# Another group order, another row stride and another operand schedule in the projection stage of a hybrid attention layer

## The chip, the core and the metric

The kernel runs on one core of a Trainium2 chip. The metric is the device time of one execution in microseconds (us). The core has five engines that run their own instruction streams and meet at semaphores: TensorE (PE, matrix products; PEld is its weight load), VectorE (DVE), ScalarE (ACT), GpSimd (POOL) and SyncE (SP), which here only issues DMA transfers. Sixteen DMA engines move the data of all transfers.

## The reference, cut to what matters

```python
def reference(x, mem, pre_norm, w_in, sink_a, mem_norm, w_mem_kv, w_out, post_norm):
    u = rms_norm(x, pre_norm)                         # (4096, 1024)
    proj = einsum('bsd,de->bse', u, w_in)             # 1024 x 3072 weights
    qa, ka, va, ga, qb, kb, vb, gb, qc, gc = split(proj, IN_SPLITS)
    # A: 6 query heads, 2 key heads, causal window 128, a sink; partial rotary on 16 of 64 dims
    # B: 6 heads, causal windows (128, 1), (512, 4), (2048, 16) as (window, dilation); partial rotary
    # C: 4 heads over 256 memory tokens, no rotary
    qa, ka, qb, kb = apply_partial_rope(...)
    ...
    y = concatenate([oa * silu(ga), ob * silu(gb), oc * silu(gc)])
    y = einsum('bse,ed->bsd', y, w_out)
    return x + rms_norm(y, post_norm)
```

All is float32, one batch, 4096 tokens, width 1024. The change touches only the first line's norm and the projection `proj`, with its rotary part and the way in which the results reach DRAM.

## The kernel before, in words

Three stages follow one another: `project_stage` (norm, projection, rotary), `attend_stage` and `finish_stage`. The first ends at 1211 us of the profiled span, and only it is changed.

**Tiles.** The stage goes through the tokens in four quarters of 1024 and, in each quarter, through the twelve groups of 256 output channels that the table `PAIRS` lists. A group is named by kind: G gate channels, R the 16 rotated dimensions of eight heads at a time (query and key), P the rest of these heads' dimensions, L those of the last four heads (rotated and not), C queries of group C, V values. Before, the order is G0 R0 G1 P0 P1 P2 L0 C0 V0 V1 G2 G3. In the text the place of a group in the quarter is i = 0 to 11, its number over all quarters is g.

**Seven products.** A group is a 256 x 1024 by 1024 x 1024 product, done as a 2 x 2 block product with seven block products instead of eight (slots j = 0 to 6). Product j multiplies an operand of the weights, W_j, and one of the tokens, U_j. U_0, U_3 and U_5 are blocks of the input, U_1, U_2, U_4 and U_6 are sums and differences that `add_u` makes in place, and U_j stays for the whole quarter. W_1, W_2, W_4 and W_5 are sums that POOL makes in the first quarter, when they are also stored to `scratch_w_s` and loaded from there in later quarters. Every operand is split into a high and a low part (`high_w`, `high_u` on ACT; `low_w`, `low_u` on DVE), and a product is 4 x 3 = 12 matmuls 128 x 128 by 128 x 512 (L807 to L809). The seven accumulate in three PSUM banks; ACT copies twice (`ps`, L477, and `p5`, L482) and DVE joins twice (L690, L695) between them. The four result blocks are called 11, 22, 12 and 21 (channel tile, token chunk).

**What sets the order.** All engines run a loop `slot(g, j)`, written out in their own code, and an engine does its work of a slot in the order of that code. `high_w(m + 2)` and `low_w(m + 2)` stand two slots ahead of their product, three buffers deep. The tables `ACT_AT` and `DVE_AT` say in which slot after a group's start its result blocks are copied to `out_a` (ring of four, ACT) and `out_b` (ring of two, DVE: `low`, L584, and the rotary steps `shuffle`, `straight`, `across`, `both`, L600 to L620). SP stores each block one slot later (`store_a`, `store_b`), and `claim_a` and `claim_b` make ACT and DVE wait until the ring's old contents have landed in DRAM. Blocks of R, P, L go to `scratch_qk_hi` and `scratch_qk_lo`, each as one DMA, or two for L, through `rows_to`. A V block is turned on PE (`turn_v`) and stored by nine DMAs (L307, L311, L314).

**The next quarter's tokens.** From i = 2 to i = 9 one tile of 128 tokens of the next quarter goes through: SP loads it to `x_next` in slot 4 of the group before (L364), ACT squares it in slot 0 (L419), DVE and ACT make the scale (`mean`, `root`, `invert`, slots 1 and 2; L562, L423, L567), ACT scales it (`scale`, slot 2, L427), PE turns it in slot 3 (L779) and DVE keeps it in slot 4 (L574). In group 11 the seven operands are replaced: `add_u` for n = 0, 1 in slots 1 and 2 of group 10, n = 2, 3 in slots 1 and 4 of group 11, `high_u` and `low_u` (L414, L546) of U_0 to U_5 in slots 1 to 6, of U_6 in slot 0 of the next quarter. Ahead of the first quarter all of this stands before slot 0.

**Last quarter.** There are no next tokens; the 256 memory tokens go through in groups 1 to 5, `differ` makes four sums of the output weights at `DIFFER_AT`, and POOL loads the first head's queries and keys when the stores are through.

## Time and profile before

| | us |
|---|---|
| median of 3 runs | 2367.25 |
| lowest and highest | 2360.48, 2370.09 |
| the profiled execution | 2361.82 |
| its span, first to last instruction | 2360.0 |
| projection stage in it | 0 to 1211 |

The page of the profile gives PE as busy for 89% of the span, PEld 74%, DVE 65%, ACT 57%, POOL 4%, and a granted TensorE clock of 0.936 on average. A matmul is pipelined, so a busy PE need not be at its peak; what counts below is how long a group of seven products takes from its first matmul to the next group's first. The timeline lists instructions in order of time with the idle time of their engine before them and what ended it; `x4` behind a row says how many alike are merged. `SPq` rows are issues of DMAs. The view of windows gives, for chosen stretches, busy times, the granted clock (1.00 is 2.4 GHz, 0.5 is 1.2 GHz) and the share of the 16 DMA engines that was busy.

### The profile page before, as it was taken

What the parts mean: (1) busy time and instruction counts of PE and PEld (TensorE: products, weight loads), DVE (VectorE), ACT (ScalarE), POOL (GpSimd) and SP (SyncE); (2) the same over time, 40 slices, a digit from 0 to 9 for tenths busy, and PEclk for the clock granted to TensorE, in tenths of its full rate; (3) what the DMA queues carried; (4) which work ended last, traced back from release to release, by engine and by line L of the source; (5) the groups of instructions that cost most, each with busy time, mean ns of one, the idle gap of its engine ahead of it and who ended that gap; (6) DMA issues with size and microseconds to landing.
All of it is one profiled execution on the core that took longest, in us unless ns stands there. A gap on an engine that the chain in (4) does not pass through costs nothing. (4 is left out here: it accounts for less than half of the span.)

```text
span 2360.0 us, 39321 instructions
## 1 busy us (share of the span) xinstructions
PE 2107.9 (89%) x12892; PEld 1754.0 (74%) x12892; DVE 1544.9 (65%) x4410; ACT 1353.5 (57%) x3520; POOL 93.1 (4%) x92
## 2 busy tenths in 40 slices
PE   4997879979899798997869999999999979899998
PEld 3776668767687576876758888888778868678886
DVE  6534455443654435534338889899889968788887
ACT  6442445534554345422249988899779969633332
POOL 0211120000000000000110000000000000000000
PEclk6998999989999899999978999899999989999999
DMA  4464565656566466565867767866959878345553
GB/s 135 151 203 155 176 199 157 218 162 195 174 189 211 151 198 198 163 230 187 239 160 142 141 121 139 165 120 129 173 115 219 198 179 214 118 161 166 168 163 124
DMA packets 429816, 401.39 MB, mean 170 GB/s; under 512 B 202128, under 2 KB 327184, under 8 KB 424768
## 3 DMA queue, kind: packets, MB, share of 16 engines
q1 hardware_dynamic: 424656, 377.38, 60.2%
q0 software_dynamic: 4976, 21.71, 2.9%
q8 instruction: 97, 1.59, 0.3%
q14 instruction: 87, 0.71, 0.1%
HBM read 255.62 MB, written 143.39 MB: 169 GB/s over the span
## 5 line engine op out<-in xcount | busy, mean ns | idle before, releaser
L807 PE MATMUL p_ps<-p_u_hi,p_w_hi 128*128 128x512 f32 x1344 | 548.2, 408 | 91.0 <-DVE p_w_lo L539 26.1
L808 PE MATMUL p_ps<-p_u_lo,p_w_hi 128*128 128x512 f32 x1344 | 537.6, 400 | 0.0
L809 PE MATMUL p_ps<-p_u_hi,p_w_lo 128*128 128x512 f32 x1344 | 537.2, 400 | 0.0
L539 DVE TENSOR_TENSOR p_w_lo<-p_w_raw,p_w_hi 128x512 fp32r<-128x512 f32 x336 | 240.1, 719 | 361.5 <-ACT p_w_hi L403 359.8
L1567 ACT ACTIVATE probs<-probs,a_stat 128x256 f32<-128x256 f32 (+1 forms) x896 | 433.7, 489 | 51.8 <-DVE a_stat L1401 48.9
L403 ACT ACTIVATE p_w_hi<-p_w_raw 128x512 fp32r<-128x512 f32 x336 | 209.1, 626 | 358.8 <-PE p_ps L809 344.9
L807 PEld LDWEIGHTS p_ps<-p_u_hi,p_w_hi 128*128 128x128 f32 x1344 | 262.4, 195 | 155.8 <-issue 58.3
L1401 DVE CUSTOM_DVE_ANT_0 probs<-a_ps_s,fixed 128x256 f32<-128x256 f32 (+1 forms) x704 | 251.8, 397 | 87.8 <-PE a_ps_s L1300 86.3
L809 PEld LDWEIGHTS p_ps<-p_u_hi,p_w_lo 128*128 128x128 f32 x1344 | 261.0, 194 | 57.1
L808 PEld LDWEIGHTS p_ps<-p_u_lo,p_w_hi 128*128 128x128 f32 x1344 | 261.9, 195 | 53.1
L1354 PE MATMUL a_ps_o<-a_pT,a_v 128*64 128x128 f32 x3320 | 259.5, 288 | 23.3 <-ACT a_pT L1591 21.7
L1370 PE MATMUL a_ps_t<-fixed,probs 128*128 128x128 f32 x1660 | 262.8, 280 | 6.3 <-ACT a_pT L1591 4.6
L1490 DVE TENSOR_SCALAR probs<-probs,a_coef 128x256 f32<-128x256 f32 (+1 forms) x896 | 263.6, 339 | 3.0
L1591 ACT ACTIVATE a_pT<-a_ps_t 128x512 f32<-128x512 f32 (+1 forms) x412 | 229.7, 561 | 40.6 <-PE a_ps_t L1370 40.3
L1354 PEld LDWEIGHTS a_ps_o<-a_pT,a_v 128*64 128x64 f32 x3320 | 184.5, 139 | 80.2 <-ACT a_pT L1591 45.3
L1299 PE MATMUL a_ps_s<-k_hi,q 128*128 128x256 f32 (+1 forms) x672 | 218.6, 343 | 7.2 <-PEq L248 3.5
L1370 PEld LDWEIGHTS a_ps_t<-fixed,probs 128*128 128x128 f32 x1660 | 197.8, 144 | 13.8 <-DVE probs L1490 8.1
L1300 PE MATMUL a_ps_s<-k_lo,q 128*128 128x256 f32 (+1 forms) x672 | 193.2, 304 | 0.0
L1567 ACT ACTIVATION_READ_ACCUMULATOR probs<-probs,a_stat 128x1 f32 x896 | 175.0, 195 | 0.0
L1299 PEld LDWEIGHTS a_ps_s<-k_hi,q 128*128 128x128 f32 x672 | 138.1, 205 | 37.2 <-issue 27.3
L2168 PE MATMUL f_ps<-f_w_lo,parts_hi 128*128 128x512 f32 x384 | 150.1, 391 | 0.0
L2167 PE MATMUL f_ps<-f_w_hi,parts_hi 128*128 128x512 f32 x368 | 144.5, 393 | 5.4 <-DVE probs L2083 4.1
(200 smaller groups left out, 2748.5 us busy)
## 6 DMA issues: line engine op xcount, KB each, us to landing
p_w_raw<-in_w_in SPq DMA_DIRECT2D x156, 256.0 KB, 3.9
p_w_raw<-scratch_w_s SPq DMA_DIRECT2D x144, 256.0 KB, 3.7
scratch_qk_hi<-p_out_a SPq DMA_DIRECT2D x80, 256.0 KB
scratch_qk_lo<-p_out_b SPq DMA_DIRECT2D x80, 256.0 KB
a_v<-scratch_v SPq DMA_DIRECT2D x40, 512.0 KB, 7.4
scratch_gate<-p_out_a SPq DMA_DIRECT2D x64, 256.0 KB
scratch_v<-p_out_a SPq DMA_DIRECT2D x256, 64.0 KB
a_gate<-scratch_gate SPq DMA_DIRECT2D x64, 256.0 KB, 5.1
```

Of the source, the lines that this page charges most:

```text
L403: nc.scalar.activation(w_hi[:, m % 3, :, :], w_raw[:, entry(j, g), :, :], ACT.Copy).then_inc(w_hi_ready, 1)
L539: nc.vector.tensor_tensor(w_lo[:, m % 3, :, :], w_raw[:, entry(j, g), :, :], w_hi[:, m % 3, :, :].bitcast(F32), ALU.subtract).then_inc(w_l ...
L807: nc.tensor.matmul(bank, hi, u_hi[j][:, k, :], start=j < 2 and k == 0, stop=False, skip_group_check=True)
L808: nc.tensor.matmul(bank, hi, u_lo[j][:, k, :], start=False, stop=False, skip_group_check=True)
L809: last = nc.tensor.matmul(bank, lo, u_hi[j][:, k, :], start=False, stop=k == KH - 1, skip_group_check=True)
L1299: nc.tensor.matmul(out, w, keys_of(keys_hi, u), start=True, stop=False)
L1354: last = nc.tensor.matmul(place_of(ps_o[j * HD:(j + 1) * HD, bank % 2, :], u), v[name][:, half, tile, :], pT[:, e % 4, j, at * P:(at + 1) ...
L1370: last = nc.tensor.transpose(ps_t[:, e % 2, j, at * P:(at + 1) * P], probs[:, s, 2 * e + j, at * P:(at + 1) * P], ident[:])
L1401: last = nc.vector.tensor_tensor_reduce(out=probs[:, s, 2 * slot + j, a:], in0=ps_s[:, slot % NS, j, a:], in1=masks[u.kind][:, a:], scale= ...
L1490: last = nc.vector.tensor_scalar(place, place, coef[:, s, u.column:u.column + 1], None, ALU.mult)
L1567: last = nc.scalar.activation(place, place, ACT.Exp, scale=-1.0, bias=stat[:, s, 0, u.column:u.column + 1], accum_out=stat[:, s, 1, u.colu ...
L1591: nc.scalar.activation(pT[:, e % 4, :, a[0]:], ps_t[:, e % 2, :, a[0]:], ACT.Copy).then_inc(turned_copied, 1)
```

## The change

1. `PAIRS` becomes G0 V0 R0 G1 P0 P1 V1 L0 P2 C0 G2 G3: the two V groups stand at i = 1 and i = 6, five groups apart, and C at i = 9. `DIFFER_AT` moves by one to two groups, and `turn_v` waits for the tiles of its own place.
2. In `rows_to` the rows of the qk scratch tensors are addressed as `(a q) n`, one stride of four rows, where they were `(h q r) n`, blocks of 16 rows. Row 4a + part holds what row 64h + 16 part + r held, for queries and keys alike, so that the dimensions of a head stand in another order in all of them. The readers are unchanged.
3. The token operands are replaced at slots 1, 3, 4, 6, 7, 9 and 10 from the start of group 11 (`U_AT`), seven operands over eleven products, on DVE one slot later; `add_u` moves with them. The square of the next tile stands in slot 6 of the group before instead of slot 0, its mean and inverse one slot earlier.
4. In the first group of all the products run in the order 0 3 1 2 4 5 6 (`FIRST`), and U_0 and U_3 are split before the last tiles are through. `number`, `u_number` and `product_at` carry that order to the semaphores.

```diff
-PAIRS = (("G", 0), ("R", 0), ("G", 1), ("P", 0), ("P", 1), ("P", 2), ("L", 0), ("C", 0), ("V", 0), ("V", 1), ("G", 2), ("G", 3))
+PAIRS = (("G", 0), ("V", 0), ("R", 0), ("G", 1), ("P", 0), ("P", 1), ("V", 1), ("L", 0), ("P", 2), ("C", 0), ("G", 2), ("G", 3))
...
-        DIFFER_AT = ((7, 6), (8, 1), (8, 4), (8, 6))
+        DIFFER_AT = ((8, 6), (9, 1), (9, 4), (9, 6))
...
+        FIRST = (0, 3, 1, 2, 4, 5, 6)
+        U_AT = {1: 0, 3: 1, 4: 2, 6: 3, 7: 4, 9: 5, 10: 6}
+
+        def product_at(g, place):
+            return FIRST[place] if g == 0 else place
+
+        def number(g, j):
+            return NJ * g + (FIRST.index(j) if g == 0 else j)
...
                     if kind == "L":
-                        by = of[2 * 512:2 * 512 + 256].rearrange("(h q r) n -> q h r n", q=4, r=16)
-                        return [(slice(HD * e, HD * e + HD), by[2 * t + e][:, :, cols]) for e in range(2)]
+                        by = of[2 * 512:2 * 512 + 256].rearrange("(a q) n -> q a n", q=4)
+                        return [(slice(HD * e, HD * e + HD), by[2 * t + e][:, cols]) for e in range(2)]
...
-                    by = of[512 * i:512 * i + 512].rearrange("(h q r) n -> q h r n", q=4, r=16)
-                    return [(slice(0, P), by[part][:, :, cols])]
+                    by = of[512 * i:512 * i + 512].rearrange("(a q) n -> q a n", q=4)
+                    return [(slice(0, P), by[part][:, cols])]
...
-                for j in (4, 6, 0, 3):
+                for j in (0, 3, 4, 6):
                     load_w(j, 0)
...
-                        act.wait_ge(raw_ready, XT * quarter + (4 if quarter == 0 and j == 0 else XT))
+                        act.wait_ge(raw_ready, XT * quarter + (4 if quarter == 0 and j < 5 else XT))
...
-                    if t == 5:
-                        high_u(0, 0)
-                for j in range(1, NJ):
+                    if t in (5, 6):
+                        high_u(0, FIRST[t - 5])
+                for j in FIRST[2:]:
                     high_u(0, j)
...
-                    if i == NP - 1 and quarter < 3 and j > 0:
-                        high_u(quarter + 1, j - 1)
-                    if i == 0 and 0 < quarter < 4 and j == 0:
-                        high_u(quarter, NJ - 1)
+                    if i == NP - 1 and quarter < 3 and j in U_AT:
+                        high_u(quarter + 1, U_AT[j])
+                    if i == 0 and 0 < quarter < 4 and NJ + j in U_AT:
+                        high_u(quarter, U_AT[NJ + j])
...
+                    if quarter < 3 and 0 <= t + 1 < XT and j == 6:
+                        n = (quarter + 1) * XT + t + 1
+                        act.wait_ge(x_loaded[0], 16 * (n - XT + 3))
+                        square(n, x_next)
                     if quarter < 3 and 0 <= t < XT:
                         n = (quarter + 1) * XT + t
-                        if j == 0:
-                            act.wait_ge(x_loaded[0], 16 * (n - XT + 3))
-                            square(n, x_next)
...
-                    if quarter < 3 and i == NP - 2 and j in (1, 2):
-                        add_u(quarter + 1, j - 1)
-                    if quarter < 3 and i == NP - 1 and j > 0:
-                        low_u(quarter + 1, j - 1)
-                        if j == 1:
-                            add_u(quarter + 1, 2)
-                        if j == 4:
-                            add_u(quarter + 1, 3)
+                    if quarter < 3 and i == NP - 2 and j in (1, 4):
+                        add_u(quarter + 1, (1, 4).index(j))
+                    if quarter < 3 and i == NP - 1 and j - 1 in U_AT:
+                        low_u(quarter + 1, U_AT[j - 1])
+                    if quarter < 3 and i == NP - 1 and j == 3:
+                        add_u(quarter + 1, 2)
...
-                product(g, j)
+                product(g, product_at(g, j))
```

The order of instructions moves at three places that matter below.

**First place: SP around the value stores, second quarter.** `scratch_v` rows are the nine stores of a V block, `p_spare<-in_x` is the load of the next tile, `p_w_raw` rows are weight loads. Before, around the first block of V0:

```order
L323 DMA scratch_qk_lo<-p_out_b 128x512 [waits p_lo_ready]
L259 DMA p_w_raw<-scratch_w_s 128x512 [waits p_w_lo_ready] x2
L364 DMA p_spare<-in_x 128x1024 [waits p_u_turned]
L259 DMA p_w_raw<-in_w_in 128x512 [waits p_w_lo_ready] x2
L259 DMA p_w_raw<-scratch_w_s 128x512 [waits p_w_lo_ready]
L307 DMA scratch_v<-p_out_a 128x4x128 [waits p_a_ready]
L311 DMA scratch_v<-p_out_a 32x4x128 x4
L314 DMA scratch_v<-p_out_a 16x8x128 x4
```

After, around the last two blocks of V1, in group L0:

```order
L319 DMA scratch_v<-p_out_a 128x4x128 [waits p_a_ready]
L323 DMA scratch_v<-p_out_a 32x4x128 x4
L326 DMA scratch_v<-p_out_a 16x8x128 x4
L271 DMA p_w_raw<-scratch_w_s 128x512 [waits p_w_lo_ready]
L319 DMA scratch_v<-p_out_a 128x4x128 [waits p_a_ready]
L323 DMA scratch_v<-p_out_a 32x4x128 x4
L326 DMA scratch_v<-p_out_a 16x8x128 x4
L271 DMA p_w_raw<-scratch_w_s 128x512 [waits p_w_lo_ready]
L376 DMA p_spare<-in_x 128x1024 [waits p_u_turned]
L271 DMA p_w_raw<-in_w_in 128x512 [waits p_w_lo_ready]
L329 DMA scratch_qk_hi<-p_out_a 64x512 [waits p_a_ready]
L329 DMA scratch_qk_hi<-p_out_a 64x512
```

The last tile's load stood ahead of the value stores; now a tile's load stands behind four blocks of nine stores, after V0 and after V1. The stores of L have a two-dimensional row pattern, 64x512, where it was 4x16x512 (and 128x512 for R and P, where it was 8x16x512).

**Second place: ACT at the start of the program**, from the split of the token operands to the first copy of a product (`p_ps<-p_ps`). Before:

```order
L414 ACTIVATE p_u_hi1<-p_spare 128x2048 [waits p_added]
L414 ACTIVATE p_u_hi2<-p_raw 128x2048 [waits p_added]
L414 ACTIVATE p_u_hi3<-p_raw 128x2048 [waits p_raw_ready]
L414 ACTIVATE p_u_hi4<-p_raw 128x2048 [waits p_added]
L414 ACTIVATE p_u_hi5<-p_raw 128x2048 [waits p_raw_ready]
L414 ACTIVATE p_u_hi6<-p_raw 128x2048 [waits p_u_turned,p_added]
L403 ACTIVATE p_w_hi<-p_w_raw 128x512 [waits p_w_added]
L477 ACTIVATE p_ps<-p_ps 128x512 [waits p_multiplied]
```

After:

```order
L427 ACTIVATE p_u_hi3<-p_raw 128x2048 [waits p_raw_ready]
L436 ACTIVATE p_ss<-p_ss 128x1 [waits p_meaned]
L440 ACTIVATE p_x_first<-p_x_first,p_ss 128x1024 [waits p_inverted]
L427 ACTIVATE p_u_hi1<-p_spare 128x2048 [waits p_added]
L427 ACTIVATE p_u_hi2<-p_raw 128x2048 [waits p_added]
L427 ACTIVATE p_u_hi4<-p_raw 128x2048 [waits p_added]
L427 ACTIVATE p_u_hi5<-p_raw 128x2048 [waits p_raw_ready]
L427 ACTIVATE p_u_hi6<-p_raw 128x2048 [waits p_u_turned,p_added]
L416 ACTIVATE p_w_hi<-p_w_raw 128x512 [waits p_w_added]
L490 ACTIVATE p_ps<-p_ps 128x512 [waits p_multiplied]
```

U_3 moved ahead of the last tile's scale; the copy of product 0 still stands behind all seven splits. On PE the second product is now that of U_3, and its first row waits for that copy (`p_products_copied`), which product 1 did not.

**Third place: DVE at the change from the first to the second quarter**, from the split of U_1 on. Before:

```order
L546 TENSOR_TENSOR p_u_lo1<-p_spare,p_u_hi1 128x2048 [waits p_added,p_u_hi_ready]
L690 TENSOR_TENSOR p_ps<-p_ps,p_p5 128x512 [waits p_products_copied,p_multiplied]
L539 TENSOR_TENSOR p_w_lo<-p_w_raw,p_w_hi 128x512 [waits p_w_hi_ready]
L546 TENSOR_TENSOR p_u_lo2<-p_raw,p_u_hi2 128x2048 [waits p_added,p_u_hi_ready]
L539 TENSOR_TENSOR p_w_lo<-p_w_raw,p_w_hi 128x512 [waits p_w_hi_ready]
L546 TENSOR_TENSOR p_u_lo3<-p_raw,p_u_hi3 128x2048 [waits p_u_hi_ready]
L557 TENSOR_TENSOR p_raw<-p_raw 128x2048 [waits p_added]
L695 TENSOR_TENSOR p_c22<-p_ps,p_p5 128x512 [waits p_a_ready,p_multiplied]
```

After:

```order
L561 TENSOR_TENSOR p_u_lo1<-p_spare,p_u_hi1 128x2048 [waits p_added,p_u_hi_ready]
L713 TENSOR_TENSOR p_c22<-p_ps,p_p5 128x512 [waits p_a_ready,p_multiplied]
L554 TENSOR_TENSOR p_w_lo<-p_w_raw,p_w_hi 128x512 [waits p_w_hi_ready]
L561 TENSOR_TENSOR p_u_lo2<-p_raw,p_u_hi2 128x2048 [waits p_added,p_u_hi_ready]
L554 TENSOR_TENSOR p_w_lo<-p_w_raw,p_w_hi 128x512 [waits p_w_hi_ready] x2
L561 TENSOR_TENSOR p_u_lo3<-p_raw,p_u_hi3 128x2048 [waits p_u_hi_ready]
L554 TENSOR_TENSOR p_w_lo<-p_w_raw,p_w_hi 128x512 [waits p_w_hi_ready]
L561 TENSOR_TENSOR p_u_lo4<-p_raw,p_u_hi4 128x2048 [waits p_added,p_u_hi_ready]
```

Between U_1's split and the second join (`p_c22`) stood two more splits and a sum; now the join comes right behind it.

## Rows read from the trace of the kernel before

**Rows 1.** Windows, L807 alone: quarters one, two, four; length, PE busy, PEclk, DMA.

```profile
35.41:357.58 322.17, 140.30 (x336) 67.81 (x337) 0.89 0.52 164
357.58:632.99 275.41, 135.64 (x337) 64.65 (x336) 0.95 0.59 182
...
910.55:1211.40 300.85, 137.16 (x336) 65.14 (x335) 0.93 0.66 204
```

**Rows 2.** Windows, single groups: R0, G1, C0, C0 (last quarter), G3 three times.

```profile
376.65:395.69 19.04, 10.89 (x28) 5.26 (x28) 1.00 0.48 153
395.69:415.65 19.96, 10.99 (x28) 5.26 (x28) 1.00 0.59 169
499.41:534.12 34.71, 11.73 (x28) 5.69 (x28) 0.80 0.43 134
1070.67:1100.63 29.96, 11.75 (x29) 5.64 (x28) 0.83 0.42 128
601.67:632.99 31.32, 12.91 (x29) 6.08 (x28) 0.84 0.54 161
321.35:357.58 36.23, 12.47 (x28) 6.11 (x28) 0.86 0.65 196
1171.05:1211.10 40.05, 12.76 (x28) 6.17 (x28) 0.74 0.66 187
```

**Rows 3.** Windows, one product each, after a stall and at full clock.

```profile
524.40:528.68 4.28, 2.39 (x4) 1.30 (x5) 0.63 0.77 223
531.40:534.12 2.72, 1.56 (x4) 0.75 (x4) 1.00 0.75 242
```

**Rows 4.** Waits over the whole span: total us, times, longest us.

```profile
DVE p_out_b L584 <- DMA scratch_qk_lo<-p_out_b: 106.9, 34, 6.8
...
PE p_ps_t L779 <- ACT p_spare L427: 63.4, 15, 14.1
...
DVE p_out_b L608 <- DMA scratch_qk_lo<-p_out_b: 48.5, 4, 13.9
```

**Rows 5.** Timeline, group C0 of the second quarter: DVE, ACT, ACT, PE.

```profile
516.27 0.69 DVE L608 COPY p_out_b<-p_ps 64x512 f32<-64x512 f32 x1 [12.09 <-DMA scratch_qk_lo<-p_out_b]
...
518.35 0.20 ACT L423 ACTIVATE p_ss<-p_ss 128x1 f32<-128x1 f32 x1 [14.90 <-DVE p_ss L562]
...
521.58 1.15 ACT L427 ACTIVATE p_spare<-p_spare,p_ss 128x1024 f32<-128x1024 f32 x1 [2.02 <-DVE p_ss L567]
...
522.78 1.11 PE L779 MATMUL p_ps_t<-p_ident,p_spare 128*128 128x128 f32 x4 [12.32 <-ACT p_spare L427]
```

**Rows 6.** Windows, all engines: while P stores run, then while only L stores run.

```profile
445.00:447.00 2.00, 2.00 (x10) 1.67 (x9) 0.72 (x4) 1.21 (x3) 0.00 (x0) 1.00 0.53 197
...
512.00:514.00 2.00, 0.00 (x0) 0.00 (x0) 0.00 (x0) 0.00 (x0) 0.00 (x0) 0.97 0.26 102
```

**Rows 7.** Timeline of SP, third of the V blocks behind V0, second quarter.

```profile
570.59 0.59 SPq L259 DMA_DIRECT2D p_w_raw<-in_w_in  x1
571.23 0.43 SPq L307 DMA_DIRECT2D scratch_v<-p_out_a  x1
...
573.77 2.46 SPq L314 DMA_DIRECT2D scratch_v<-p_out_a  x4
```

**Rows 8.** Page, DMA issues: count, KB each, median us to landing.

```profile
p_spare<-in_x SPq DMA_DIRECT2D x24, 512.0 KB, 4.2
```

**Rows 9.** Timeline of the program's start: DVE, DVE, ACT, PE.

```profile
52.72 6.69 DVE L546 TENSOR_TENSOR p_u_lo<-p_raw,p_u_hi 128x2048 fp32r<-128x2048 f32 x3
59.33 1.89 DVE L539 TENSOR_TENSOR p_w_lo<-p_w_raw,p_w_hi 128x512 fp32r<-128x512 f32 x3
...
52.84 1.91 ACT L414 ACTIVATE p_u_hi<-p_raw 128x2048 fp32r<-128x2048 f32 x1 [1.49 <-DVE p_raw L557]
...
60.12 0.77 PE L807 MATMUL p_ps<-p_u_hi,p_w_hi 128*128 128x512 f32 x1 [9.27 <-DVE p_w_lo L539]
```

**Rows 10.** Timeline of ACT in the last group of the stage.

```profile
1191.63 0.60 ACT L444 ACTIVATE p_out_a<-p_ps 128x512 f32<-128x512 f32 x1 [15.84 <-DMA scratch_v<-p_out_a]
```

68 lines of the change are left out of this document (39 added, 29 removed).

## The prediction

> **What bounds the kernel now.** I read the windows first, a quarter at a time and then a group at a time, because the busy share of PE says little about a stage with many short stalls. A group without anything beside its seven products takes 19.04 us, 2.72 us a product, and one that also turns a tile of the next tokens takes 19.96 us, both at a granted clock of 1.00 [rows 2]. Twelve groups, eight of them with a tile, are 12 x 19.04 + 8 x 0.92 = 235.8 us, and the turning of the two V groups' blocks adds an estimated 4 us, so that an undisturbed quarter is about 240 us. The quarters took 322, 275 and, the last one, 301 us [rows 1]; the third was like the second. Some 14 us of the last are the memory tokens' own products. So about 205 us of the 1176 us from the first product to the end are stalls and the slow clock behind them, and PE is what waits. In the stretches of single groups most of this sits at three places: C0 (35 us in the second quarter, 30 in the last, where 19 to 20 would do), G3 (31, 36 and 40 us) and the start [rows 2, 9]. The two other stages are not changed, and their 1149 us are taken as they are.
>
> A stall costs more than its length: the product after one took 4.28 us at a mean clock of 0.63, where the next but one took 2.72 at 1.00 [rows 3]. I add 1.6 us to each stall over about 2 us.
>
> **Part 1, the row stride.** In C0 PE waits 12.32 us for ACT's scale of the next tile, ACT has waited 14.90 us for DVE's mean, and DVE 12.09 us for the buffer whose last content, an L block's low part, was still on its way to DRAM [rows 5]. Why it was: in a stretch in which only L stores run, 0.26 of the DMA engines' time is busy, 4.2 of sixteen engines, at 102 GB/s, which is 24 GB/s an engine; with P stores it is 0.53, 8.5 engines [rows 6]. The patterns had 4 and 8 as their outer size. Half an L block is 128 KB, so four engines take 1.35 us for it, an L group's 16 halves 21.5 us, all on the same four, issued within some 14 us. With 64 or 128 rows as the outer size I take sixteen engines: 128 KB in 0.34 us, a P block in 0.67 us instead of 1.33. The Trainium skill, "DMA: Bandwidth & Descriptors", section "Why a DMA increments its semaphore by 16 and not by 1", says that a transfer is split over the largest number up to 16 that divides the outer size on both sides; the trace agrees for the 4 and the 8, and by that rule the new patterns get 16, while by the bounds of rows 6 alone they get between 4 and 16. Two sums come off. The four C0 groups exceed their floor by 15, 14.8, 15 and 10.9 us (36 less 20, and so on), 56 us, of which two are in rows 2. The other waits of the turn: 63.4 us in 15 waits, less three in C0 of 14.1, 12.3 and about 12, leave 25 [rows 4, 5]; with the clock behind six of them 35. DVE's 107 us of short waits for these stores [rows 4] are what fed them, and the earlier square and mean (one slot, 2.72 us) help the same chain; I leave 6 us of the 35. Gain: 56 + 29 = 85 us, if nothing takes the place of the waits.
>
> **Part 2, the value groups apart.** A V block is nine DMA issues: from 571.23 to 576.23 SP issues nothing else, and with the weight load ahead of it a block takes 5.7 us of SP [rows 7]. A slot is 2.72 us. Eight blocks in a row put SP some 20 us behind, and G3 pays: in the last quarter ACT waits 15.84 us there for a V block's store, and G3 takes 40 us for 19 [rows 10, 2]. I put the lag's share at 22 us there, 10 in the first quarter, 7 each in the two between (the rest of their excess is part 3). Behind a single V group SP lags about as far at its end but has catch-up time before a ring is full. Gain: 46 us.
>
> What it triggers: SP now loads a tile behind the four blocks (the first order excerpt). The first block is issued about 2 us before the following group begins, four blocks and four weight loads are 22.8 us, so the tile's load is issued at about 21.5 us into that group and lands 4.2 us later [rows 8], at about 26. ACT's square of it stands in slot 6, at about 18 us, and ACT is in order: queued behind it are the weight splits and the copy that product 2 of the next group needs. That product would start at about 26.5 us; it gets its copy at 26 + 1.1 (square) + 1.7 to 2.3 (a split, one or two block copies, the copy itself) = 29 to 29.5. Stall 3 us and the clock, 4 to 5 us, at six places: R0 and L0 of three quarters. In the first quarter the weight sums are not loaded by SP, the lag is 2 us shorter, and R0 costs 1. In L0 the lag meets a second wait: L's first low block is stored about 29 us into the group, and DVE wants its buffer at 25.5 until it lands at 32. The two overlap; I take 5 us for L0 in each of four quarters and 4, 4 and 1 for R0. Cost: 29 us. Bounds: 0, if SP drains in time, and 65, if each of the seven costs the 9 us by which the wait for a slow landing could grow.
>
> **Part 3, seven operands over eleven products.** A split of an operand is 6.69 / 3 = 2.2 us on DVE, a weight split 0.63, and 1.9 us on ACT [rows 9]. Before, seven splits and two sums, nine times 2.2, with seven weight splits and two joins (5.7 us), are 25.5 us of DVE in 19 us of G3: 6.5 us too much. That agrees with G3's 31.3 less 19.0 less the 7 of part 2. Over the ten slots from 2 to 11 the same nine, ten weight splits and four joins are 28.7 us in 27.2, and DVE may run 4 us late on the weight splits. The joins have 2 us of slack. The first two splits and the sum push the second join about 1 us past it, so I leave 2 us at each of three changes. Gain: 19 - 6 = 13 us.
>
> **Part 4, the start.** DVE's chain ahead of slot 0 stays what it was: seven splits, four sums, eight tiles, and the third product began at 60.12 when it was through [rows 9]. The split of U_3 fills 2 us in which DVE waited for the last tile, but U_2's high part now stands between two of DVE's steps and costs them back. The second product needs the copy of product 0, which ACT reaches only after all seven splits (second excerpt), at about 58.4: product 1 ran at 46 to 50 before, product 3 cannot now. It takes 4.5 us at half clock, so the third product starts at 63 instead of 60, and the join of product 1 comes one slot nearer. The rest catches nothing up but DVE's own lag of 1 us. Cost: 2 us, between 0 and 5.
>
> **Edits at no cost.** The memory tokens' ACT wait in group 1 of the last quarter stays, now in V0. `differ` moves to P2 and C0, whose DVE has 0.7 us more work a slot; its own spacing is the same, and so is its wait for the transfers; up to 3 us if that cover is gone. The permuted rows are read in the same whole rows by the later stages.
>
> **Sum.** 85 + 46 + 13 - 29 - 2 = 113 us off the profiled execution's 2361.82: 2249 us. The median of the three runs is 5.4 us above that execution; with half of it for the changed kernel's median I predict 2251 us.
>
> **Rivals.** *The tile loads are in time.* If SP's lag is a few us shorter or the stores, now on all engines, land sooner, the square does not wait and L0 costs half: 26 us less, 2225 us. For it: the weight loads in rows 7 are only one a block. Against it: nothing shortens the nine issues. *The tile loads cost double.* With ACT blocked, a split, a copy and the join come late one after another, as in G3 before: 29 more, 2280 us. *The stores do not spread*, or rows 64 KB apart are written more slowly than rows 16 KB apart: the change does not do what it says. Then the 85 us stay away and only parts 2 to 4 count: 46 + 13 - 2 - 9 (R0) = 48, 2314 us. For it: no row before shows such a row distance; against it: with an outer size of 8 the engines kept 24 GB/s each at rows 1 MB apart between engines. *Slower than before.* The new ACT wait for a tile's load at the six places is the mechanism. The gains without it are 142 us; to be over by 12 us it has to cost over 25 us a place, so a tile would land about 48 us into the group. It decides if the weight loads behind the same lag arrive late as well, so that PE waits first for them and SP for PE's weights again: 27 us a place gives 2362 - 142 + 162 = 2382 us. Against it: in G3, with twice as many blocks, the whole excess was 12 to 21 us.
>
> **Chances.** The forecast 0.58, tiles in time 0.18, tiles double 0.13, no spread 0.08, slower 0.03. About 12 us, 0.5%, is what a measurement of this kernel can tell from no change. All cases but the last are faster by more; I leave 0.02 for a sum of small losses that ends level. The range is 2212 to 2292: it takes in the first three cases with some 12 us for the sizes of parts 1 and 2, and leaves out the no-spread case.
>
> **What would show it.** Part 1: windows with L stores at a DMA share well over 0.26; DVE's waits for `scratch_qk_lo` from 155 us to under 50; PE's waits for ACT's scale under 15 us; C0 near 20 us. Part 2: G3 of the last quarter near 20 us, and in its place a wait of ACT's square (now L432) for `p_spare<-in_x` in R0 and L0 of 5 to 8 us, six times. Part 3: G3 and the G0 behind it together near 40 us, with PE's idle time there by the join. Part 4: the second product at 58 us, group 0 ending near 77. The quarters would be near 278, 254, 254 and 271 us. Wrong would be a DMA share that stays at 0.26 under L stores, or no wait of ACT for tiles, or G3 still over 25 us.

## The result, and the profile after

| | before | after |
|---|---|---|
| median of 4 runs | 2363.86 us | 2241.4 us |
| lowest and highest | 2357.76, 2370.09 | 2240.56, 2245.04 |
| the profiled execution | 2361.82 | 2240.56 |
| its span | 2360.0 | 2238.8 |
| first product to last product of the projection | 35.4 to 1211.6 | 35.5 to 1084.5 |

The ratio of after to before is 0.9485, 95% interval 0.9455 to 0.9515: 122 us or 5.2% faster. The prediction was 2251 us, range 2212 to 2292. All twelve runs below are timed beside the kernel before; its median in the three sets was 2365.5, 2363.2 and 2364.5 us, the last without one execution of 2439.65 us that had a lower granted clock (0.82) and stands in no ratio.

Line numbers have moved, and each run below has those of its own kernel. In the changed kernel the square is L432, the mean L577, the reciprocal L582, ACT's scale L440, PE's turn of a tile L797, `straight` L623, `low` L599, the copy of product 0 L490, the join L708.

The first view is of windows, with the matmuls of L825 alone: length, busy PE, busy PEld, granted clock, DMA share, GB/s. The rows are the four quarters; then C0 of the second and of the last quarter; G3 of the second and of the last; G1 and P2 of the second, P2 of the third and of the first.

```profile
35.52:315.50 279.98, 135.90 (x337) 65.03 (x337) 0.95 0.58 186
315.50:564.94 249.44, 133.90 (x337) 63.78 (x336) 0.99 0.65 203
564.94:815.84 250.90, 133.99 (x336) 63.79 (x336) 0.99 0.64 201
815.84:1084.10 268.26, 134.65 (x336) 64.11 (x335) 0.97 0.70 224
506.42:526.35 19.93, 10.98 (x28) 5.26 (x28) 1.00 0.80 263
1025.08:1045.54 20.46, 10.97 (x29) 5.25 (x28) 1.00 0.82 298
545.39:564.94 19.55, 10.97 (x29) 5.26 (x28) 1.00 0.46 139
1065.34:1084.10 18.76, 10.89 (x28) 5.07 (x27) 1.00 1.02 253
376.23:398.06 21.83, 11.07 (x28) 5.25 (x28) 1.00 0.73 228
479.76:506.42 26.66, 12.34 (x29) 5.94 (x28) 0.87 0.73 227
731.33:757.30 25.97, 11.78 (x28) 5.56 (x28) 0.93 0.73 232
224.88:255.43 30.55, 12.32 (x28) 6.00 (x28) 0.89 0.69 196
```

Read beside [rows 1, 2]: C0 went from 34.7 and 30 us to 19.9 and 20.5, G3 from 31.3 and 40 to 19.6 and 18.8, both at full clock. The quarters took 280, 249, 251 and 268 us where the prediction had 278, 254, 254 and 271. Group 0 of the first quarter takes 41.3 us, and in the last quarter V0 takes 27.4 and P0 32.9 us beside the work on the memory tokens, much as R0 and P1 did before (26.7 and 32.9 us). What else is left over the 19.96 us of a plain group with a tile sits in P2 (6 to 10.6 us, in every quarter) and in G1 (5.4, 1.9 and 4.0 us in the first three). These are the two groups that follow R0 and L0, and R0 and L0 are the groups that follow the single V groups.

The second view is of the waits over the whole span: total us, times, longest.

```profile
ACT p_spare L432 <- DMA p_spare<-in_x: 37.7, 8, 7.4
DVE p_out_b L599 <- DMA scratch_qk_lo<-p_out_b: 42.0, 20, 4.6
DVE p_out_b L623 <- DMA scratch_qk_lo<-p_out_b: 22.3, 4, 8.7
PE p_ps_t L797 <- ACT p_spare L440: 4.0, 2, 3.0
PE p_ps L825 <- ACT p_ps L490: 34.5, 7, 18.8
```

DVE's waits for the low parts' stores fell from 155 us [rows 4] to 64, PE's waits for a scaled tile from 63.4 to 4.0, and ACT no longer waits for the stores of V blocks ([rows 10] had 15.84 us of it in one place). In their place stands ACT's wait for the next tile, 37.7 us, of which 37.0 are the six waits behind the V groups, 4.0 to 7.4 us each.

The third view is the timeline around L0 and P2 of the second quarter (P2 begins at 479.76): the fourth V block and the tile's load on SP, ACT's square, PE's third product of P2, DVE's ring. SPq L319, L323 and L326 are the nine issues of a V block.

```profile
474.31 0.43 SPq L319 DMA_DIRECT2D scratch_v<-p_out_a  x1
474.78 2.02 SPq L323 DMA_DIRECT2D scratch_v<-p_out_a  x4
476.85 4.05 SPq L326 DMA_DIRECT2D scratch_v<-p_out_a  x4
480.95 0.59 SPq L271 DMA_DIRECT2D p_w_raw<-scratch_w_s  x1
481.58 0.44 SPq L376 DMA_DIRECT2D p_spare<-in_x  x1
...
484.83 1.13 SPq L335 DMA_DIRECT2D scratch_qk_lo<-p_out_b  x2
485.29 1.06 ACT L432 ACTIVATE p_spare<-p_spare 128x1024 f32<-128x1024 f32 x1 [7.36 <-DMA p_spare<-in_x]
...
487.86 0.58 ACT L490 ACTIVATE p_ps<-p_ps 128x512 f32<-128x512 f32 x1
...
488.59 0.77 PE L825 MATMUL p_ps<-p_u_hi,p_w_hi 128*128 128x512 f32 x1 [3.23 <-ACT p_ps L490]
...
493.53 0.69 DVE L623 COPY p_out_b<-p_ps 64x512 f32<-64x512 f32 x1 [3.82 <-DMA scratch_qk_lo<-p_out_b]
```

The tile is loaded 22.9 us after L0 began (the prediction said 21.5, and a landing at 26; ACT's square starts as it lands, 26.6 us after), ACT's in-order queue holds the split and the copy behind the square, and PE stalls 3.23 us (the prediction said 3), then runs this product and the next at a lower clock. At the end of the stage stands something that the prediction left out. The timeline has POOL's first load of the next stage's queries and PE's first matmul of that stage, behind a barrier:

```profile
1059.78 0.53 POOL L933 DMA_DIRECT2D q<-scratch_qk_hi  x1 [11.48 <-DMA scratch_qk_lo<-p_out_b]
...
1092.88 0.44 PE L1318 MATMUL a_ps_s<-k_hi,q 128*128 128x128 f32 x1 [8.33 <-PEq L260]
```

The barrier opens when all engines are through, and the last are SP and POOL: the last gate store landed at 1091.9 us and the last of POOL's loads at 1091.2. Both share the DMA engines (the DMA share over G3 is 1.02). SP's last wait ahead of the barrier, in the view of its waits, is for those stores:

```profile
SPq L399 <- DMA scratch_gate<-p_out_a: 6.4, 1, 6.4
```

### The profile page after: what moved, and what is told of

It is laid out like the page before. It is cut to its first block and busy times, and to the rows that moved or that the text cites. A ratio compares the mean times of both kernels' runs of the same rounds, so it can differ in the third digit from the quotient of the medians.

```text
span 2238.8 us, 39324 instructions
## 1 busy us (share of the span) xinstructions
PE 2071.6 (93%) x12892; PEld 1730.7 (77%) x12892; DVE 1546.8 (69%) x4410; ACT 1352.4 (60%) x3520; POOL 95.8 (4%) x92
## 5 line engine op out<-in xcount | busy, mean ns | idle before, releaser
L825 PE MATMUL p_ps<-p_u_hi,p_w_hi 128*128 128x512 f32 x1344 | 538.4, 401 | 53.9 <-ACT p_ps L490 34.5
L827 PE MATMUL p_ps<-p_u_hi,p_w_lo 128*128 128x512 f32 x1344 | 530.1, 394 | 0.0
L826 PE MATMUL p_ps<-p_u_lo,p_w_hi 128*128 128x512 f32 x1344 | 529.7, 394 | 0.0
L825 PEld LDWEIGHTS p_ps<-p_u_hi,p_w_hi 128*128 128x128 f32 x1344 | 256.8, 191 | 114.8 <-DVE p_w_lo L554 26.9
L827 PEld LDWEIGHTS p_ps<-p_u_hi,p_w_lo 128*128 128x128 f32 x1344 | 256.2, 191 | 55.1
L826 PEld LDWEIGHTS p_ps<-p_u_lo,p_w_hi 128*128 128x128 f32 x1344 | 256.9, 191 | 51.3
L1373 PE MATMUL a_ps_o<-a_pT,a_v 128*64 128x128 f32 x3320 | 259.1, 288 | 22.5 <-ACT a_pT L1610 20.7
```

What stands on the lines that cost most here:

```text
L825: nc.tensor.matmul(bank, hi, u_hi[j][:, k, :], start=j < 2 and k == 0, stop=False, skip_group_check=True)
L826: nc.tensor.matmul(bank, hi, u_lo[j][:, k, :], start=False, stop=False, skip_group_check=True)
L827: last = nc.tensor.matmul(bank, lo, u_hi[j][:, k, :], start=False, stop=k == KH - 1, skip_group_check=True)
L1373: last = nc.tensor.matmul(place_of(ps_o[j * HD:(j + 1) * HD, bank % 2, :], u), v[name][:, half, tile, :], pT[:, e % 4, j, at * P:(at + 1) ...
```

## The experiments

**Part 1 alone.** The kernel before with the two new lines of `rows_to`.

```diff
-    by = of[2 * 512:2 * 512 + 256].rearrange("(h q r) n -> q h r n", q=4, r=16)
-    return [(slice(HD * e, HD * e + HD), by[2 * t + e][:, :, cols]) for e in range(2)]
+    by = of[2 * 512:2 * 512 + 256].rearrange("(a q) n -> q a n", q=4)
+    return [(slice(HD * e, HD * e + HD), by[2 * t + e][:, cols]) for e in range(2)]
```

> The kernel before with part 1 alone: the blocks of R, P and L go to rows of one stride, the order of the groups, the operands and the start are those of before. My theory (the stores of L ran on four engines and held DVE's ring, which made the square's mean, ACT's scale and PE's turn late): C0 of the middle quarters falls from 34.7 us to about 20, the DMA share while L blocks are stored rises over 0.5, and the time is 2362 less 56 (C0) less 25 to 40 (the other waits for a scaled tile) = 2266 to 2281 us. Rival (L directly ahead of C0 is what costs, whatever the rate, because each L block is two transfers and the ring has two places): C0 stays at 25 us or more, and no more than 60 us are gained, 2302 us or more.

Measured: 2281.64 us (2275.95 to 2283.14), ratio 0.9633 (0.9583 to 0.9682). 84 us are gained, and the time is 0.6 us over the range that I expected; the prediction had 85 for this part. Windows, all engines, of C0 in the second quarter, and 2 us inside it in which L blocks are stored (the last three numbers are clock, DMA share, GB/s):

```profile
466.62:491.68 25.06, 21.77 (x94) 17.84 (x92) 12.65 (x23) 10.57 (x19) 0.00 (x0) 0.93 0.64 191
...
471.00:473.00 2.00, 2.00 (x11) 1.65 (x10) 0.38 (x1) 0.00 (x0) 0.00 (x0) 1.00 0.92 306
477.00:479.00 2.00, 0.66 (x3) 0.20 (x2) 1.24 (x3) 0.73 (x2) 0.00 (x0) 1.00 0.00 0
```

With a weight load beside the L stores the DMA share is 0.92 at 306 GB/s, where [rows 6] had 0.26 at 102, and a few us later nothing is in flight. In the changed kernel there is a stretch in which the transfers in flight are L stores alone:

```profile
490.60:491.79 1.19, 1.19 (x5) 0.91 (x4) 0.00 (x0) 0.00 (x0) 0.00 (x0) 0.50 0.85 257
```

The stretches of [rows 6] were not quite that. In the one with P stores two weight loads were in flight, and in the one with L stores one, which had been issued behind the L stores at 506.86 us and landed only at 516.85, 10.0 us later. The weight load behind L stores in the run with part 1 alone took 3.0 us (472.35 to 475.32). So transfers that fill a few DMA engines also hold up a later one that needs those engines among others.

C0, however, stays at 25 us, as the rival said: DVE still waits 3.05 us for the ring there, with the mean behind it. Over its four groups C0 gives 37 us (8.1, 9.7, 9.7, 9.6) where I had 56, and the other groups give 46 where I had 29. Each theory was right about one of the two.

**Part 1 undone.** The changed kernel with the old lines of `rows_to`, the diff above reversed.

> The changed kernel with the row stride of before (outer size 4 for L, 8 for R and P), all else as changed. My theory: the waits for the low parts' transfers come back behind L0, P2 and C0 wait for scaled tiles, and 50 to 85 us of the gain go: 2290 to 2325 us, with a DMA share of 0.26 while only L blocks are stored. Rival (the new order of groups alone, with P2 between L0 and C0, gives DVE the time that it lacked): under 25 us are lost, 2265 us or less.

Measured: 2346.96 us (2340.72 to 2357.99), ratio 0.9928 (0.9902 to 0.9954). 106 us are lost, over the upper end of what I expected, and the kernel is within 1% of the one before. Windows of P2 in the second quarter, and 2 us inside it:

```profile
524.61:562.70 38.09, 24.54 (x93) 19.71 (x92) 11.50 (x21) 11.02 (x20) 0.00 (x0) 0.78 0.45 151
543.00:545.00 2.00, 0.00 (x0) 0.00 (x0) 0.00 (x0) 0.00 (x0) 0.00 (x0) 0.51 0.26 102
```

P2 takes 43.5, 38.1, 37.0 and 36.8 us, C0 28, 24, 25 and 31. No engine works in that window: the four DMA engines hold everything. DVE's wait at L623 is 61.3 us in four places (22.3 in the changed kernel). The stride is worth more in the new order than in the old (106 us against 84). My reading is that L0 now stands behind a V group and its stores begin late as well; no run parts this from the rest. This run is also the case "the stores do not spread" of the prediction, which priced it at 2314 us. Without part 1 the other parts bring some 18 us and not the 48 of that case.

**Same rows, another pattern.** The changed kernel with the same addresses written as two sizes.

```diff
-    by = of[2 * 512:2 * 512 + 256].rearrange("(a q) n -> q a n", q=4)
-    return [(slice(HD * e, HD * e + HD), by[2 * t + e][:, cols]) for e in range(2)]
+    by = of[2 * 512:2 * 512 + 256].rearrange("(h r q) n -> q h r n", q=4, r=16)
+    return [(slice(HD * e, HD * e + HD), by[2 * t + e][:, :, cols]) for e in range(2)]
```

> The changed kernel with every block going to exactly the same rows as in it, but with the rows written as a pattern of two sizes, 4 x 16 for L and 8 x 16 for R and P, instead of 64 and 128. If the number of engines follows the outer size of the pattern, the DMA share under L stores is 0.26 again and the time is that of the kernel with the old stride within 5 us (2290 to 2325). If it follows the addresses, or the two sizes are merged on the way, the time is that of the changed kernel, 2241 within 5 us.

Measured: 2245.77 us (2237.88 to 2248.41), ratio 0.948 (0.9429 to 0.953), the changed kernel's 0.9485. Two microseconds with L stores in P2 show 0.97 of the DMA engines busy:

```profile
488.00:490.00 2.00, 1.64 (x8) 1.02 (x6) 0.00 (x0) 1.24 (x3) 0.00 (x0) 1.00 0.97 336
```

Weight loads are in flight beside them here too. So it is not how the pattern is written in the source that counts, but whether the rows lie at one distance. Whether two sizes of one stride are merged before the transfer is issued, or the split goes by the addresses, this run can't tell.

**Part 2 undone.** The old group order in the changed kernel.

```diff
-PAIRS = (("G", 0), ("V", 0), ("R", 0), ("G", 1), ("P", 0), ("P", 1), ("V", 1), ("L", 0), ("P", 2), ("C", 0), ("G", 2), ("G", 3))
-DIFFER_AT = ((8, 6), (9, 1), (9, 4), (9, 6))
+PAIRS = (("G", 0), ("R", 0), ("G", 1), ("P", 0), ("P", 1), ("P", 2), ("L", 0), ("C", 0), ("V", 0), ("V", 1), ("G", 2), ("G", 3))
+DIFFER_AT = ((7, 6), (8, 1), (8, 4), (8, 6))
```

> The changed kernel with the group order of before (V0 and V1 side by side ahead of G2, L0 ahead of C0), all else as changed: part 2 undone alone. My theory: SP's lag comes back in G3, 22, 10, 7 and 7 us (46 in all), C0 behind L0 costs 25 us again as with the stride alone (5, 5 and 8 over its floor, 18 us), and the stalls in G1 and P2 behind the single V groups go (35 us by the trace of the changed kernel): 2241 + 46 + 18 - 35 = 2270 us, between 2258 and 2282. Rival (setting the V groups apart moves the same SP lag from G3 to R0 and L0 and wins nothing): 2246 us or less, with G3 over 25 us and G1 and P2 at 20.

Measured: 2252.57 us (2248.13 to 2254.43), ratio 0.9532 (0.9507 to 0.9556): 11 us slower than the changed kernel, between the two expectations. As a time that is no more than a measurement here can tell; the groups of the two traces say where it sits. Windows, all engines, of G3 in the last, first, second and third quarter, then C0 of the second:

```profile
1060.21:1099.60 39.39, 21.57 (x83) 17.00 (x84) 5.55 (x8) 7.87 (x14) 10.63 (x15) 0.78 0.67 188
284.83:317.03 32.20, 22.36 (x85) 17.67 (x85) 16.64 (x14) 15.85 (x20) 5.91 (x4) 0.79 0.67 209
539.74:563.67 23.93, 21.17 (x86) 16.74 (x84) 14.05 (x13) 14.46 (x18) 0.00 (x0) 0.93 0.64 201
785.46:811.04 25.58, 21.13 (x85) 16.73 (x84) 14.06 (x13) 14.48 (x18) 0.00 (x0) 0.93 0.65 196
455.67:476.98 21.31, 20.39 (x94) 16.55 (x93) 11.52 (x21) 10.61 (x19) 0.00 (x0) 1.00 0.78 222
```

G3 costs 20.6, 12.6, 4.4 and 6.0 us more than in the changed kernel, 43.6 in all (46 predicted), and G1 and P2 cost 43 us less. So SP's lag was moved and not removed, and both sides are of one size. The rest that makes the new order win is small: C0 behind L0 costs 4.4 and 1.4 us in the first two quarters, V0 of the last quarter, where the four sums collide with it, 7 us; and 5 us go back at the end of the stage, which the old order passes in 3.5 us and the new one in 8.3.

**Part 3 undone.** The operands replaced one a slot again.

```diff
-U_AT = {1: 0, 3: 1, 4: 2, 6: 3, 7: 4, 9: 5, 10: 6}
+U_AT = {1: 0, 2: 1, 3: 2, 4: 3, 5: 4, 6: 5, 7: 6}
```

with `low_u` in the same slot as `high_u` and the sums at their old places.

> The changed kernel with the operands of the next quarter replaced as before, one a slot in G3 and the last in slot 0 of G0: part 3 undone alone. My theory (DVE has 25.5 us of work in 19 us of G3): G3 goes from 19.6 us to 24 to 26 at the three changes of quarter, G0 behind it from 19.8 to 19.0, and the time is 2241 + 3 x 5 = 2256 us, between 2251 and 2262. Rival (the stalls in G3 were SP's lag alone, and with that gone DVE's extra work hides in the slack ahead of the joins): 2245 us or less.

Measured: 2260.55 us (2253.51 to 2264.89), ratio 0.9573 (0.954 to 0.9607); its profiled execution has a span of 2254.9 us, 16 more than the changed kernel's. Windows of G3 and of the G0 behind it:

```profile
554.69:579.87 25.18, 21.21 (x86) 16.76 (x85) 20.69 (x16) 17.49 (x19) 0.00 (x0) 0.93 0.35 97
579.87:598.90 19.03, 19.03 (x85) 15.76 (x84) 10.87 (x12) 9.57 (x16) 0.00 (x0) 1.00 0.57 175
```

5.6 us in G3 less 0.8 in G0, three times, are 14.4 us (13 predicted), with 3.5 more in G2 of the first quarter and 0.4 in each of the other two. DVE is busy 20.7 of the 25.2 us, and PE waits for its joins (2.89 and 1.08 us). The theory holds.

**Part 4 undone.** The start of before: `FIRST = (0, 1, 2, 3, 4, 5, 6)`, the splits and sums in their old order, the weights loaded in the order 4, 6, 0, 3.

> The changed kernel with the start of before (products 0, 1, 2, 3 in that order in group 0, the splits and sums in their old order, the weight blocks loaded in the old order): part 4 undone alone. My prediction put part 4 at a cost of 2 us, between 0 and 5: 2239 us, with the second product at 46 us, the third at 60 and group 0 ending at 75. Rival (the new order helps what follows group 0): 2244 us or more.

Measured: 2239.5 us (2238.28 to 2245.02), ratio 0.9481 (0.9458 to 0.9504). The second and third products start at 45.5 and 59.3 us and group 0 ends at 75.0, as expected; it takes 40.4 us (41.3 in the changed kernel). Parts of 2 us can't be told from no change here; that it costs 2 us agrees with the prediction and is not shown.

**The tile's load moved forward.** `load_next` is the load of the tile as it was, made a function.

```diff
+    if g < G and j == 2 and g and kind_of(g - 1) == "V":
+        load_next(g)
     ... the stores of the slot ...
-    if quarter < 3 and 0 <= t < XT and j == 4:
+    if j == 4 and not (g and kind_of(g - 1) == "V"):
         load_next(g)
```

> The changed kernel with one issue moved on SP: behind a V group (in R0 and L0) the next tile is loaded in slot 2, between the second and the third V block, instead of in slot 4 behind all four. My theory (ACT's square waits for that load, 37.7 us in 8 waits, and the copy that PE needs is queued behind it): the square waits no more, G1 falls from 25.4, 21.8 and 23.9 us to 20, P2 from 30.6, 26.7 and 26.0 to 22 to 24, where the wait of DVE for the ring of L stays; 2241 - 22 = 2219 us, between 2211 and 2227. Rival (SP's lag of four blocks is what costs, through the weight loads and the ring of L as well; another wait takes the place of this one): under 10 us, 2231 us or more.

Measured: 2258.58 us (2256.68 to 2269.6), ratio 0.9555 (0.9501 to 0.9608). It is 17 us slower than the changed kernel. Another wait took the place of the one removed, as the rival had it, but neither expectation had a loss. Timeline of L0 and P2 in the second quarter (P2 begins at 491.78): PE's turn of the tile before, the load behind it, L's first low block, DVE's wait for the ring:

```profile
482.73 1.03 PE L804 MATMUL p_ps_t<-p_ident,p_spare 128*128 128x128 f32 x8
483.80 0.36 SPq L365 DMA_DIRECT2D p_spare<-in_x  x1
...
500.66 1.11 SPq L335 DMA_DIRECT2D scratch_qk_lo<-p_out_b  x2
...
508.04 0.69 DVE L630 COPY p_out_b<-p_ps 64x512 f32<-64x512 f32 x1 [11.50 <-DMA scratch_qk_lo<-p_out_b]
```

ACT no longer waits for a tile. But the tile's buffer is free only when PE has turned the tile before, so SP stood still for 3 us with two V blocks behind it, L's first low block went out 29.9 us after L0 began instead of 26.1, and DVE's wait for the ring grew from 3.8 to 11.5 us. P2 took 31.2 us instead of 26.7, and now the scale waits for the reciprocal behind that ring.

**The load ahead of the fourth block only, the scale's inputs first.** The same edit at `j == 3`, by when PE has turned the tile, and on DVE:

```diff
+    if g < G and quarter < 3 and 0 <= i - X_AT < XT:
+        if j == 0:
+            mean((quarter + 1) * XT + i - X_AT)
+        if j == 1:
+            invert((quarter + 1) * XT + i - X_AT)
     for age in (2, 1, 0):
```

> The changed kernel with two edits against the stalls in G1 and P2: the tile behind a V group is loaded in slot 3, ahead of the fourth V block only (PE has turned the tile before it by then, so SP need not wait as it did in slot 2), and DVE makes the mean and its reciprocal at the head of slots 0 and 1, ahead of its waits for the ring of L. My theory now: in the run with the load in slot 2 SP waited 3 us for the turn, L's first low block went out 4 us later, and DVE's wait for the ring grew from 3.8 to 11.5 us with the reciprocal behind it, so ACT's scale and PE's turn were late. With both edits P2 falls from 26.7 to 21 to 23 us and G1 to 20: 2241 - 20 = 2221 us, between 2213 and 2229. Rival (what binds is SP's total lag; the ring of L then stops DVE's join instead): 2236 us or more.

Measured: 2236.3 us (2231.43 to 2241.29), ratio 0.9462 (0.9436 to 0.9488): 5 us under the changed kernel, within what can't be told from no change. Windows of G1 and P2 in the second quarter, of the run:

```profile
379.01:398.98 19.97, 19.97 (x94) 16.60 (x93) 16.18 (x29) 12.64 (x22) 0.00 (x0) 1.00 0.83 258
480.67:508.18 27.51, 23.09 (x93) 18.75 (x92) 13.26 (x24) 10.94 (x21) 0.00 (x0) 0.88 0.71 213
```

What stops PE in that P2, in the timeline:

```profile
497.01 0.77 PE L833 MATMUL p_ps<-p_u_hi,p_w_hi 128*128 128x512 f32 x1 [4.42 <-DVE p_ps L715]
```

G1 is at its floor in the second and third quarters, so there the tile's load was its whole stall. In the first it takes 27.8 us (25.4 in the changed kernel), and PE waits 5.07 us in it for DVE's second join: there another wait takes the tile's place. In P2 nothing is won: the wait of ACT and the late scale are gone, and DVE's first join, behind the same ring, is late. The rival was right there.

**The gate group behind V1.** Order G0 V0 R0 G1 P0 P1 V1 G2 L0 P2 C0 G3.

```diff
-DIFFER_AT = ((8, 6), (9, 1), (9, 4), (9, 6))
+DIFFER_AT = ((6, 6), (7, 1), (7, 4), (7, 6))
```

> The changed kernel with one more change of the group order: G2 stands behind V1, then L0, P2, C0, G3, and the four sums of the output weights are made in G2 (slots 1, 4 and 6 and the last slot of V1) instead of P2 and C0. My theory (P2's stall of 6 to 10 us in every quarter comes from L0 standing directly behind V1: SP issues L's first low block 26 us after the group began, since four V blocks are ahead of it, and the ring of two is full): with the gate group behind V1, which puts nothing into that ring, P2 falls to 20 to 21 us in all four quarters, 10.6, 6.7, 6.0 and 9 us less, and G2 stays within 2 us of its 20: 2241 - 30 = 2211 us, between 2203 and 2220. Rival (the lag only moves: ACT waits in G2 for the V blocks' stores as it did in G3 of before): G2 at 24 us or more and 2225 us or more.

Measured: 2266.79 us (2263.72 to 2274.43), ratio 0.9602 (0.9573 to 0.963), 25 us slower than the changed kernel. My expectation missed; the rival's bound on the time holds, but not its G2 of 24 us. Windows of G2, L0 and P2 in the second quarter:

```profile
469.57:490.60 21.03, 21.03 (x103) 17.45 (x101) 7.51 (x12) 11.37 (x19) 0.00 (x0) 1.00 0.69 187
490.60:515.41 24.81, 21.57 (x93) 17.49 (x92) 11.15 (x19) 10.91 (x18) 0.00 (x0) 0.93 0.63 198
515.41:536.46 21.05, 20.42 (x93) 16.55 (x92) 12.88 (x24) 9.53 (x17) 0.00 (x0) 1.00 0.72 200
```

The timeline of POOL's first load for the next stage and of PE's wait at the barrier:

```profile
1087.18 0.53 POOL L933 DMA_DIRECT2D q<-scratch_qk_hi  x1 [70.65 <-DMA scratch_qk_lo<-p_out_b]
...
1118.95 0.44 PE L1318 MATMUL a_ps_s<-k_hi,q 128*128 128x128 f32 x1 [20.48 <-PEq L260]
```

P2 does fall as expected (21 to 25.8 us in the first three quarters, 20.4 in the last), and G2 stays at 21. I had left out three things. V1's lag is met one group later: L0 costs 3 to 6.5 us over a plain group, in the first three quarters by ACT's wait for the tile, and in the last, which has no tile, by ACT's waits for the V blocks' stores (3.92 and 5.74 us), the rival's wait at another place. G3 of the first quarter takes 26.7 us instead of 19.6, with 5.64 us of DVE's wait for the ring in it, since C0 now stands directly ahead. With smaller losses elsewhere the stage ends 14 us later, although P2 is 24 us shorter in all. And C0's low parts are now the last to be stored: POOL, which waits for all stores of queries and keys, begins its loads at 1087 us, 11 us ahead of the stage's end at 1098.5. SP was through at 1110.6 us, the last of POOL's loads landed at 1117.3, and then the barrier opened; it costs 20.5 us. The loads alone keep the DMA engines busy, as the window between the two shows, in which no engine works:

```profile
1110.60:1117.00 6.40, 0.00 (x0) 0.00 (x0) 0.00 (x0) 0.00 (x0) 0.00 (x0) 0.50 0.84 201
```

**The start mixed.** ACT and DVE do slots 0 to 4 of group 0 between the splits of U_1, U_2, U_4, U_5 and U_6.

```diff
-for j in FIRST[2:]:
-    high_u(0, j)
+for place, j in enumerate(FIRST[2:]):
+    high_u(0, j)
+    slot(0, place)
```

That is the edit on ACT; DVE's is alike.

> The changed kernel with the start alone altered: ACT and DVE do the first five slots' work of group 0 (weight splits, copies, the first join) between the splits of the token operands instead of behind all of them. My theory (the second product waits 18.8 us for a copy that ACT makes behind all seven splits, and from the third product on DVE's splits of the weights come behind all of DVE's): the second product starts at 50 us instead of 58, the third at 55, and the last at 66 instead of 74, because DVE's chain of sums and splits, which ends at 59, now also carries 5 us of other work: 7 us less, 2234 us, between 2229 and 2239. Rival (DVE's chain sets the end either way): under 2 us.

Measured: 2241.81 us (2235.19 to 2248.56), ratio 0.9492 (0.9462 to 0.9521). The second product starts at 48.3 us and group 0 takes 38.3 us, 3 less, where I expected 7 and the rival under 2: the fifth product now waits 4.32 us for the first join, which stands behind a split. Those 3 us are not in the time, which lies over my range; G1 of the first quarter took 28.8 us in this trace, 25.4 in the changed kernel's.

**All of it.** The four edits above that I held for gains, and the memory tokens' load one slot earlier.

> All that I hold for gains together: the gate group behind V1, the mixed start, the tile behind a V group loaded ahead of the fourth V block, mean and reciprocal at the head of DVE's slots, and the memory tokens' load one slot earlier. From the changed kernel's 2241 us: 30 for P2, 7 for the start, 11 for G1 (5.4, 1.9 and 4.0 over its 20 us), 3 for V0 of the last quarter: 2190 us, between 2178 and 2203. Rival (SP's queue is full and the gains overlap): 2210 us or more.

Measured: 2241.95 us (2234.88 to 2251.23), ratio 0.9495 (0.9465 to 0.9525), 52 us over what I expected; the rival's bound holds. The stage itself ends at 1068.7 us, 16 us earlier than in the changed kernel. The barrier takes 12 of them back: POOL's loads begin at 1057.4, again behind C0, and the last of them lands at 1087.8 (the timeline of this run, whose profiled execution, 2234.88 us, was the fastest of the six):

```profile
1057.37 0.53 POOL L940 DMA_DIRECT2D q<-scratch_qk_hi  x1 [70.90 <-DMA scratch_qk_lo<-p_out_b]
...
1089.47 0.45 PE L1325 MATMUL a_ps_s<-k_hi,q 128*128 128x128 f32 x1 [20.80 <-PEq L260]
```

**The changed kernel again**, beside these three.

> The changed kernel itself, on the chip of the three runs beside it, so that they can be compared with it without the kernel before between them: 2241 us, within 5.

Measured: 2241.02 us (2233.39 to 2249.56), ratio 0.948 (0.9448 to 0.9512). No version here beats it by more than a measurement can tell.

## Why the prediction was right, and where it was right by luck

**What bounds the kernel.** The floor of 240 us a quarter, with the stalls read as what is over it, held: the second and third quarters now take 249 and 251 us. That a stall costs the clock as well is in the tables above (0.87 in P2, 1.00 in C0 behind it).

**Part 1.** 84 us measured alone against 85. The mechanism is shown by the DMA share (0.26 with the old rows, 0.85 with L stores alone and 0.92 beside a weight load with the new) and by the run with the old rows (106 us lost). The Trainium skill, "DMA: Bandwidth & Descriptors", section "Why a DMA increments its semaphore by 16 and not by 1", has the transfer split over the largest number up to 16 that divides the outer size on both sides. The shares agree with it: 0.26 of sixteen engines is 4.2, and 0.85 to 0.97 is 13.6 to 15.5, which is more than eight. The two terms of the sum were mis-sized against each other: C0 gave 37 instead of 56, the other groups 46 instead of 29. That the errors of -19 and +17 cancel is luck. The step "the four C0 groups exceed their floor by 56 us, and all of it goes" failed, because a ring of two places with two transfers a block still waits about 3 us at sixteen engines; that remainder went with the earlier square, mean and reciprocal and the new order (C0 is 24.3, 21.3, 20.4 and 20.3 us in the run with the old order). The other term was too small because it was priced by PE's waits for a scaled tile, with 1.6 us for the clock behind six of them. V0 alone gave 6.5, 4.8, 4.6 and 3.2 us, 19 in all, for 8.9 us of such waits, and P1, P2 and L0 of the first quarter gave 16 for 10.9; what else stood behind those stalls the runs do not part.

**Part 2.** The gain was 43.6 us in G3 against 46. The new wait came where it was put, with its cause and nearly its times. Its price was 43 us against 29: R0's places 5.4, 1.9 and 4.0, less the 1.6 that G1 of the first quarter costs in the old order too, 9.7 against 9, as said; L0's 10.6, 6.7, 6.0 and 10.0, 33 against 20. The failed step is "the two overlap; I take 5 us for L0". They overlap only in part: when ACT waits no more, DVE's ring wait stops the scale, and when the scale is taken from behind it, it stops the join. In the last quarter there is no tile at all, and P2 still takes 29 us: DVE waits 8.7 us for the ring, and PE 6.9 us for the first join behind it.

**Part 3.** 14.4 us at the three changes of quarter, 16 between the spans and 19 between the medians, against 13. The leftover of 2 us a change was 1.3 (39.4 us for G3 and G0 together, less 19.04 twice). **Part 4.** Second product at 57.95 us (58 said), group 0's end at 76.84 (77 said), for the reason given, an 18.8 us wait for the copy; the price is 2 us or nothing.

**What was left out.** "The two other stages are not changed, and their 1149 us are taken as they are": they are 1154. Only the work is unchanged, not its start. C0 now stands nearer to the end, the first head's loads begin 25 us before the end of the stage instead of 76, and PE waits 8.3 us at the barrier instead of 3.5. The barrier waits for all of those loads to land, not only for the queries that POOL's code waits for: in the traces of seven kernels POOL's last instruction of the stage ends 1.2 us after its last load has landed (1191.26 and 1192.45 in the kernel before, 1117.33 and 1118.52 with the gate group behind V1). The stage alone gained 127 us; 122 arrived.

**The sum.** Taken away one at a time, the parts are worth 106, 11, 19 and -2 us, 134 in all for 122 together: they overlap, and the prediction added them as if they did not (85, 46 - 29 = 17, 13 and -2, 113). Its own quarters add to 119 us of gain, so a few us of its agreement are chance.

**The rivals.** Tiles in time: not so, ACT waited for tiles, 37.7 us in eight waits. Its price was also added up wrongly: nothing in R0 and half in L0 take 9 + 10 = 19 us off the cost of 29 and not 26, so that it stood for 2232 us and not 2225. (Likewise seven times 9 us are 63 and not 65, and the chances add to 1 without the 0.02 for a level end.) Tiles double: nearer to the truth at L0 than the forecast, but not at R0. No spread: excluded by the DMA share. Slower: the wait did not grow over 7.4 us, and the list of ACT's waits has none for the DMA of a weight load. Of what should have shown each step, two numbers were missed: DVE's waits for the low parts are 64 us and not under 50, which is L0's ring again, and the six waits for a tile are 4.0 to 7.4 us and not 5 to 8.

## To carry to other kernels

Read the DMA share in a stretch where only one kind of transfer runs: a share near a quarter of the engines with everything else idle means that the transfer uses few engines. Here rows at one distance raised it to 0.85 and more. A queue that issues in order moves its lag when the groups are set in another order; price both places, and look at what else shares the queue behind it, since taking away one of two overlapping waits can make the other longer than both were. A stage's gain counts only as far as the next stage's first loads can start earlier: ask which store they wait for, and how long they take to land.

## What the runs showed that I had not expected

A load moved ahead of two V blocks in SP's queue cost 17 us (2258.6 against 2241.4), because it then waited for its buffer and held the 18 issues of those blocks behind it. The same rows written as 4 x 16 instead of 64 gave the same DMA share, 0.97, so the source's pattern is no guide to the number of engines. And the loads for the next stage took 30 us in both kernels with C0 directly ahead of G3 (1087.2 to 1117.3 us with the gate group behind V1, 1057.4 to 1087.8 with all edits), at a DMA share of 0.84 and more throughout. So a stage that ended 16 us earlier gained little, and the barrier grew from 8.3 to 20.8 us.
